# Small loads moved from ScalarE's DMA queue to SyncE's, and the first weight panel behind the tables

## The reference, cut to what matters

```
silu_c, silu_cc = silu(c), silu(c_ctx)
h = ctx
for l in range(2):
    mx = split(silu_c  @ w_mod[l] + b_mod[l], 6)      # shifts, scales, gates
    mc = split(silu_cc @ w_mod[l] + b_mod[l], 6)
    zx = rms_norm(x, norm1_g[l]) * (1 + mx[1]) + mx[0]
    zc = rms_norm(h, norm1_g[l]) * (1 + mc[1]) + mc[0]
    p, pc = zx @ w_in[l], zc @ w_in[l]                # nine panels of 256 columns
    # retention heads | windowed attention with sinks | chunked gating: s = w_s @ norm(v) + b_s
    x = x + mx[2] * (concat(heads) @ w_out[l])
    x = x + mx[5] * swiglu(norm2 and modulation of x)
    if l == 0: the same for h, with mc
return rms_norm(x, final_norm_g)
```

## Time and profile before

| | |
|---|---|
| device time, median of 3 runs | 1864.01 us (1863.4 to 1868.9) |
| the profiled execution's own time | 1868.9 us |
| its span, first to last instruction | 1866.8 us |
| mean granted TensorE clock, share of full speed | 0.935 |
| TensorE busy | 1661.7 us (89% of the span) |
| loads on ScalarE's queue (q10) | 0.61 MB of 155.23 MB |

### The profile page before, as it was taken

One profiled execution on the slowest core, in us unless ns is written; L12 is line 12 of the kernel. 1 busy time (PEld: TensorE's weight loads), 2 busy tenths in 40 slices (PEclk: granted clock), 3 DMA queues, 4 the chain that ended last, 5 costly groups with the idle time before them and its releaser, 6 DMA issues.

```text
span 1866.8 us, 22912 instructions
## 1 busy us (share of the span) xinstructions
PE 1661.7 (89%) x9310; PEld 1346.0 (72%) x9310; DVE 699.7 (37%) x1108; ACT 541.1 (29%) x849; POOL 515.6 (28%) x231
## 2 busy tenths in 40 slices
PE   5889985788989999999999998996689799999998
PEld 3667763456777888888888887775457678788786
DVE  3442254662432232232222354435653423423325
ACT  4212224652243111111111125233542522222223
POOL 2612231001214232322323211233003354444431
PEclk9889997779989999999999998898799899999998
DMA  8534430000224322223333110221001223232221
GB/s 293 172 124 136 136 112 1 1 1 24 84 74 158 113 91 91 79 79 112 112 112 100 58 46 23 68 68 46 1 1 50 86 80 123 67 109 93 67 90 46
DMA packets 122193, 155.23 MB, mean 83 GB/s; under 512 B 20352, under 2 KB 89872, under 8 KB 122128
## 3 DMA queue, kind: packets, MB, share of 16 engines
q1 hardware_dynamic: 120448, 153.70, 25.5%
q10 hardware_dynamic: 1680, 0.61, 0.1%
HBM read 152.21 MB, written 2.10 MB: 83 GB/s over the span
## 4 chain that ended last, share of the span: by engine, by line
PE 79%; DVE 10%; ACT 5%; issue 3%; DMA 2%; POOL 1%; SPq 0%; DVEq 0%; ACTq 0%; POOLq 0%
PE ps L1518 16%; PE ps L1519 15%; PE ps L1520 15%; PE ps L1830 5%; PE ps L1831 5%; PE ps L1832 5%; PE ps L1716 2%; PE ps L1443 2%; PE ps L1738 2%; DVE s_at L1289 1%; DVE hl L1382 1%; PE ps L1754 1%; PE ps L1451 1%; PE ps L1849 1%; PE ps L1850 1%
## 5 line engine op out<-in xcount | busy, mean ns | idle before, releaser
L437 POOL TENSOR_TENSOR wl<-raw,wh 128x1024 fp32r<-128x1024 f32 x144 | 352.9, 2463 | 839.1 <-ACT wh L541 839.1
L1518 PE MATMUL ps<-zh,wh 128*128 128x512 f32 (+1 forms) x1568 | 563.4, 359 | 13.3 <-POOL zl L437 5.7
L1519 PE MATMUL ps<-zl,wh 128*128 128x512 f32 (+1 forms) x1568 | 560.3, 357 | 0.0
L1520 PE MATMUL ps<-zh,wl 128*128 128x512 f32 (+1 forms) x1568 | 556.2, 355 | 0.0
L1518 PEld LDWEIGHTS ps<-zh,wh 128*128 128x128 f32 x1568 | 298.4, 190 | 90.3 <-issue 36.3
L1520 PEld LDWEIGHTS ps<-zh,wl 128*128 128x128 f32 x1568 | 297.7, 190 | 43.9
L1519 PEld LDWEIGHTS ps<-zl,wh 128*128 128x128 f32 x1568 | 298.3, 190 | 40.7
L541 ACT ACTIVATE wh<-raw 128x1024 fp32r<-128x1024 f32 x144 | 148.3, 1058 | 373.1 <-PE ps L1520 260.7
L1395 DVE SCALAR_TENSOR_TENSOR xT<-ps,modcol,xT 128x512 f32<-128x512 f32 (+1 forms) x264 | 169.3, 661 | 103.4 <-PE ps L1832 99.9
L1376 DVE TENSOR_TENSOR hf<-gs,ps 128x512 f32<-128x512 f32 x66 | 37.5, 596 | 408.7 <-ACT gs L873 408.6
L1830 PE MATMUL ps<-hh,wh_d 128*128 128x512 f32 x480 | 173.9, 362 | 13.4 <-DVE xT L1395 13.3
(11 more groups left out here) (232 smaller groups left out, 1723.4 us busy)
## 6 DMA issues: line engine op xcount, KB each, us to landing
raw<-in_w_gate_dram SPq DMA_DIRECT2D x22, 1024.0 KB, 7.0
raw<-in_w_up_dram SPq DMA_DIRECT2D x22, 1024.0 KB, 9.4
raw_m<-in_w_mod_dram SPq DMA_DIRECT2D x22, 1024.0 KB, 5.0
raw_d<-in_w_down_dram SPq DMA_DIRECT2D x20, 1024.0 KB, 5.0
raw<-in_w_in_dram SPq DMA_DIRECT2D x14, 1024.0 KB, 5.4
raw<-in_w_mod_dram SPq DMA_DIRECT2D x11, 1024.0 KB, 5.2
raw_n<-in_w_mod_dram SPq DMA_DIRECT2D x9, 1024.0 KB, 5.2
raw<-in_w_out_dram SPq DMA_DIRECT2D x32, 256.0 KB, 4.3
```

What stands on the lines that cost most here:

```text
L437: nc.gpsimd.tensor_tensor(dst, src, hi.bitcast(F32), ALU.subtract).then_inc(sem(done), 1)
L1518: MM(dst, wt_h[:, h, w], zh[:, k, c0:c1], start=(k == 0), stop=False)
L1519: MM(dst, wt_h[:, h, w], zl[:, k, c0:c1], start=False, stop=False)
L1520: last = MM(dst, wt_l[:, h, w], zh[:, k, c0:c1], start=False, stop=(k == KC - 1))
```

## The change

Three things are done. The ten small loads are taken out of ScalarE's stream and put into SyncE's, behind p4; the eight loads of `bsb` are put right behind them and count on the same semaphore. Whoever waited for the ten now waits for all eighteen, and the wait for `bsb` in `gate` goes. The load of rv, which stood between p6 and p7, goes through `load_in(0, 0)` and is issued behind p7 and the three tables; it keeps a wait for `use_mod` of 1, which is long fulfilled there. It is the same transfer into the same buffer.

```
@@ SyncE
             for q in range(5):
                 startup_panel(q)
-            for q in range(5, 8):
-                sp.wait_ge(sem("use_mod"), q - 2)
-                startup_panel(q)
-                if q == 6:
-                    sp.dma_start(raw[0][:, :]..., win_v[0][:, :, PANEL_COL["rv"]:PANEL_COL["rv"] + 256])...
-            for to, of, n in (...three tables...): sp.dma_start(K[:, to:to + n], ...)
+            rows = 0
+            for v, n in (norm1_g 16, norm2_g 16, final_norm_g 8, ret_norm_g 4, cm_norm_g 4):
+                sp.dma_start(rows_a[rows:rows + n, :], v).then_inc(sem("ld_small"), 16)
+                rows += n
+            sp.dma_start(rows_b[:, :], b_mod...).then_inc(sem("ld_small"), 16)
+            sp.dma_start(dec[:, 0:8], ...partition_broadcast(P)).then_inc(sem("ld_small"), 16)
+            sp.dma_start(dec[:, 8:16], ...partition_broadcast(P)).then_inc(sem("ld_small"), 16)
+            sp.dma_start(sinkb[:, :], ...partition_broadcast(P)).then_inc(sem("ld_small"), 16)
+            sp.dma_start(cws[:, :, :], cm_w_s...).then_inc(sem("ld_small"), 16)
             for l in range(DEPTH):
                 for g in range(4):
                     sp.dma_start(bsb[64 * (g % 2):64 * (g % 2) + 64, l, g // 2, :],
-                                 cm_b_s[l, g].partition_broadcast(64)).then_inc(sem("ld_bsb"), 16)
+                                 cm_b_s[l, g].partition_broadcast(64)).then_inc(sem("ld_small"), 16)
+            for q in range(5, 8):
+                sp.wait_ge(sem("use_mod"), q - 2)
+                startup_panel(q)
+            for to, of, n in (...three tables...): sp.dma_start(K[:, to:to + n], ...)
...
+            load_in(0, 0)
             load_modb(0)
@@ ScalarE
             nc.scalar.activation(csil[:, :, 1], crow[:, 1, :], ACT.Silu).then_inc(sem("csil_rdy"), 1)
-            (the ten act.dma_start of rows_a, rows_b, dec, sinkb, cws)
@@ VectorE, log_decay_a
-                dve.wait_ge(sem("ld_small"), 16 * 10)
+                dve.wait_ge(sem("ld_small"), 16 * 18)
@@ VectorE, gate
-                    dve.wait_ge(sem("ld_bsb"), 16 * 8)
@@ TensorE
-            pe.wait_ge(sem("ld_small"), 16 * 10)
+            pe.wait_ge(sem("ld_small"), 16 * 18)
```

More of the change, by code:

```diff
@@ L285, in _ @@
                 startup_panel(q)
+            rows = 0
+            for v, n in ((norm1_g.rearrange("l (k p) -> (l k) p", p=P), 16), (norm2_g.rearrange("l (k p) -> (l k) p", p=P), 16),
+                         (final_norm_g.rearrange("(k p) -> k p", p=P), 8), (ret_norm_g.rearrange("l (k p) -> (l k) p", p=P), 4),
+                         (cm_norm_g.rearrange("l (k p) -> (l k) p", p=P), 4)):
+                sp.dma_start(rows_a[rows:rows + n, :], v).then_inc(sem("ld_small"), 16)
+                rows += n
+            sp.dma_start(rows_b[:, :], b_mod.rearrange("l (k p) -> (l k) p", p=P)).then_inc(sem("ld_small"), 16)
+            sp.dma_start(dec[:, 0:8], ret_decay_f.rearrange("l h -> (l h)").partition_broadcast(P)).then_inc(sem("ld_small"), 16)
+            sp.dma_start(dec[:, 8:16], ret_decay_b.rearrange("l h -> (l h)").partition_broadcast(P)).then_inc(sem("ld_small"), 16)
+            sp.dma_start(sinkb[:, :], attn_sink.rearrange("l h -> (l h)").partition_broadcast(P)).then_inc(sem("ld_small"), 16)
+            sp.dma_start(cws[:, :, :], cm_w_s.rearrange("l g p q -> p (l g) q")).then_inc(sem("ld_small"), 16)
+            for l in range(DEPTH):
+                for g in range(4):
+                    sp.dma_start(bsb[64 * (g % 2):64 * (g % 2) + 64, l, g // 2, :],
+                                 cm_b_s[l, g].partition_broadcast(64)).then_inc(sem("ld_small"), 16)
             for q in range(5, 8):
@@ L289, in _ @@
                 startup_panel(q)
-                if q == 6:
-                    sp.dma_start(raw[0][:, :].rearrange("p (k n) -> p k n", k=KC),
-                                 win_v[0][:, :, PANEL_COL["rv"]:PANEL_COL["rv"] + 256]).then_inc(sem("ld_in0"), 16)
             for to, of, n in ((S_MASK, K_MASK, 1152), (S_DIST, K_DIST + 384, P), (S_RC, K_RC, 2 * SX)):
                 sp.dma_start(K[:, to:to + n], consts[:, of:of + n]).then_inc(sem("ld_tables"), 16)
-            for l in range(DEPTH):
-                for g in range(4):
-                    sp.dma_start(bsb[64 * (g % 2):64 * (g % 2) + 64, l, g // 2, :],
-                                 cm_b_s[l, g].partition_broadcast(64)).then_inc(sem("ld_bsb"), 16)
             def a_free(a, first=False):
@@ L618, in _ @@
             nc.scalar.activation(csil[:, :, 1], crow[:, 1, :], ACT.Silu).then_inc(sem("csil_rdy"), 1)
[L619 to L629, removed]
             for k in range(KC):
```

## The result

The changed kernel takes 1874.96 us in the median of 6 runs (1870.12 to 1878.1), the kernel before 1864.32 (1861.42 to 1868.9). The ratio is 1.0052, with a 95% interval of 1.0035 to 1.0068: slower, by 10.6 us (6.5 to 12.7). The forecast was 7.7 us more than before, 1871.7.

The account below looks back on a forecast made before the run. TensorE, busy 89% of the span, bounds the kernel, so a later first product with w_in delays everything. Norm +8.5 and rv -0.8 give +7.7 us on the median 1864.0: 1871.7 us, range 1865 to 1877.

Parts of the forecast that it names:

- T, the last small load, at 32.0: At the start, the last of the eighteen small loads lands at 32.0 us, range 28.5 to 34.8.
- the transfer bound of 31.5: SyncE's loads transfer in order behind p4, so the last small load lands at 31.5 us.
- The queue behind the wait: On TensorE, transposes, p0, p1, norm's sums and everything up to the first product wait for the small loads; norm +8.5 us.
- The clock, T + 5.9: TensorE's clock is low after standing: norm's sums start 5.9 us after the last small load lands, 3.3 at high clock.
- rv behind p7 and the tables: -0.8: Before the first product, p7 and zl come sooner with rv issued later, giving back 0.9 us at most, 0.8 taken.
- the bound of 1.1 for a late rv: Before the first product, rv landing 2 us later than reckoned costs 1.1 us instead of giving time back.
- the microsecond that the prediction named as a sign of being wrong: Prediction is wrong if rv's landing leaves more than a microsecond of TensorE's time behind it.
- Nothing behind the first product: Each microsecond the first product comes later is one of the whole time; nothing behind it gives it back.
- The hidden loads: Rival: small loads slip in among the panels, norm doesn't move; -0.8 us, 1863.2 us, chance 0.06.
- a clock that holds: Rival at the start: only issue time counts and the clock stays high; +1.5 us, 1865.5 us, chance 0.32.
- Issue time: By SyncE's issue alone, the last small load lands at 28.5 us at the earliest; used by a rival, chance 0.32.
- the held issue: Rival: SyncE's issue is held, last small load lands at 34 to 35; +10.5 us, 1874.5 us, chance 0.17.

Follow-up runs that it names:

- the ten alone: The kernel before, with only the ten small loads moved to SyncE behind p4: 1871.65 us, ratio 1.0038.
- rv alone: The kernel before, with only the load of rv moved directly behind p7 and the tables, ahead of bsb: 1865.1 us, ratio 1.0007.
- The ten ahead of p0: The kernel before, with the ten small loads moved to SyncE in front of the first panel, p0: 1864.7 us, ratio 1.0001.
- rv back: The changed kernel, with the load of rv back between p6 and p7: 1873.7 us, ratio 1.0054.
- norm first: The changed kernel, with the small loads' wait and transposes behind p0, p1 and the norm's sums; ScalarE and VectorE also take norm work first: 1870.6 us, ratio 1.0031.
- the filled wait: The changed kernel, with 54 further unread transposes of xin on TensorE ahead of its wait for the small loads: 1873.7 us, ratio 1.0048.

## Why the prediction came out as it did

The range, 1865 to 1877, and the sign were right, the size somewhat small: +10.6 against +7.7. Step by step:

- **T, the last small load, at 32.0.** The number was right: L1486 starts at 31.46, 31.52 and 32.12. That it was is in part luck, for the way there was another. The prediction leant on the transfer bound of 31.5. In the changed kernel the chain runs through SyncE's issues: p4's ended 4.6 us sooner, not 2.3, the eighteen then took 15.2 us instead of 10.35, because SyncE was held at the first `rows_a` (2.6 us for one issue) and the first `bsb` (4.3), and the last landed 2.5 us after its issue began. The errors nearly cancel. The order of the queue was right: of the eighteen, the last issued ended the wait.
- **The queue behind the wait.** Right, and shown by putting the norm in front of it. With the ten alone the norm's 3.65 us arrived whole at the first product.
- **The clock, T + 5.9.** Right: the norm's sums start 4.85, 5.90 and 5.44 us after L1486, not the 3.3 of the high clock. TensorE runs there without a gap, so the lower level costs 1.6 to 2.6 us at this place. Together with T the norm is 7.65 us later in the mean (29.45 to 37.1), where +8.5 was predicted.
- **rv behind p7 and the tables: -0.8.** This is the step that failed, in the term "this part gives back 0.9 us at most". From the norm's sums to the first product it was 29.1 us before and 30.2 after, so it costs 1.1. rv alone showed 1.1 to 1.3, and the bound of 1.1 for a late rv had been given. It is also just over the microsecond that the prediction named as a sign of being wrong. The gain could not come, since the earlier landing of p7, read as a post of the chain, doesn't bring the first `zl` forward: the run with rv between p7 and the tables has p7 1.2 us sooner after its issue than the first trace of before, and the first product where it was. And three sizes were wrong. p7 landed 5.8 us after its issue, not 4.4. rv landed 9.5 us after its own, not 8.1. GpSimd's two halves took 5.37 us, not 4.65; the second overlapped VectorE's first `zl`.
- **Nothing behind the first product.** Missed in part: by the 1001st matmul 2.1 us more have gone in all three traces, with a piece of the lower clock that the kernel before doesn't have. That nothing behind gives the delay back was right. How much of the 2.1 reaches the end the scatter doesn't show.
- **The rivals.** The hidden loads are out, and so is a clock that holds. Issue time did set T, but held issues made it 31.5 and not 28.5. The +10.6 is the +10.5 of the held issue by number, but not by its sum: T was not 34 to 35. The ten ahead of p0 show what the hidden loads would have taken.

The sum with measured terms: 7.65 + 1.1 = 8.8 at the first product, and 2.1 behind it, 10.9 against the 10.6 of the medians. The interval of 6.5 to 12.7 would hold the 8.8 alone as well.

What stays open is why the changed kernel loses the high clock at 165. Several kernels with the ten on SyncE show the same there, the one with the ten ahead of p0 too, whose first product is 1.5 us earlier than before and whose time is the same. Others with the ten on SyncE (rv back, norm first) don't, and rv alone, with the ten on ScalarE's queue, does (at 157 to 161). So neither the later start nor the queue nor rv's place explains it by itself, and no run here separates what does. Nor was the high clock ever kept over the small loads' wait, since the filled wait ran dry.

## What to carry to other kernels

A load that an engine waits for early belongs ahead of the bulk loads in its queue. Which queue it is matters less: ten small loads cost no time ahead of five panels of 1 MB and 7.5 us behind them, 3.7 of it at the first product. Before joining loads under one semaphore, ask who waits for it first and which of the joined loads that engine doesn't need: `bsb`, needed late, held TensorE's first transposes for 3 us. And count for a wait what stands behind it in the engine's stream, with the lower clock that follows when TensorE has stood. Before counting a gain from an earlier load, look at how long the instructions behind it take when the other engines are idle: 0.17 us for `acol` here, and up to 1.83 beside GpSimd.

## What the runs showed of the hardware that I had not expected

- SyncE's issues of the same size take very different times. p3's took 0.51 us and p4's 5.32, right behind each other, and the first `bsb` 4.3 us where the others took 0.6. What holds them no run here shows.
- GpSimd and VectorE hold each other up, by whole instructions. This is read from the overlap in the traces and not tried by itself. In each of the seven traces with rv in time VectorE's `acol` ends 0.02 to 0.04 us after a GpSimd instruction, whether it took 0.45 or 1.83 us until then. In the kernels where rv is late, GpSimd's second half takes 3.05 us instead of 2.35 and VectorE's first `zl` 1.46 instead of 0.96: `zl` is issued beside GpSimd's first half and ends 0.8 us behind it, and the second half ends 0.7 later than it did elsewhere.
- With ScalarE's queue empty, `x` and `ctx` land 1.0 to 1.6 us sooner (first transpose at 12.3 to 12.9 instead of 13.9; 13.7 to 14.1 in all kernels with the ten on ScalarE's), though ScalarE's loads were only 0.61 MB.
- Two executions of the same kernel differ by up to 8 us, and TensorE's clock goes with it: of the changed kernel's runs the one with a mean granted clock of 0.934 took 1878.1 us, that with 0.939 took 1870.1.
